# Layer norm's scale, offset and modulation applied where the turned tile is copied; overflow comparison outside its loop; last combine weighed on PE

## The chip, the cores and the metric

The kernel runs on one core of one Trainium2 chip. It is one program of 2,900 lines written engine by engine: TensorE (PE), VectorE (DVE), ScalarE (ACT), GpSimd (POOL) and SyncE (SP) each have their own instruction stream, and they meet at semaphores. The metric is the device time of one execution in microseconds; lower is better. The kernel before takes 4826.23 us, the median of three runs (4824.58 to 4827.52).

## The reference

All data is float32; a sequence of 1024 tokens of width 1024. Two blocks of two layers each follow one another. In the first block a layer is a mixer of delta-rule and gated linear attention heads, a product with `w_out`, and a layer norm. In the second a layer is an attention (a neighbourhood attention, then one with grouped queries), a layer norm, a mixture of 32 experts of which each token uses 2, and a layer norm. What matters here is the norm with the modulation behind it, and how the experts' results are put together:

```python
def layer_norm_2(x, g, b):
    mu = xf.mean(-1, keepdims=True)
    var = jnp.square(xf - mu).mean(-1, keepdims=True)
    return (xf - mu) * lax.rsqrt(var + LN_EPS) * g + b
...
sh1, sc1, g1, sh2, sc2, g2 = jnp.split(mod[:, None, :], 6, axis=-1)
h = x * (1 + sc1) + sh1
y = attention(h)
x = layer_norm_2(ALPHA * x + (1 + g1) * y, ln_g[i, 0], ln_b[i, 0])
h = x * (1 + sc2) + sh2
y = hierarchical_moe(h, ...)        # sum over 2 experts of gate * expert(h)
x = layer_norm_2(ALPHA * x + (1 + g2) * y, ln_g[i, 1], ln_b[i, 1])
```

The reference's experts work on blocks of 128 rows; the kernel gives each expert one block, and the blocks beyond those 32 are overflow.

## The kernel before, in words

`program` calls stage after stage. Each stage is one block in which all engines run their own streams; `end_stage` closes it with a barrier of all engines. The order of the work inside a stage is written out by hand: each engine's loop over the eight token tiles of 128 rows (`order` is 0, 4, 1, 5, 2, 6, 3, 7 in the out stages), and the semaphores between them.

**`out_stage`** runs twice, after each layer of the first block. PE multiplies a tile's mixed heads, already turned (`m.mixT`), with `w_out` in `m.xT` (L1410): 16 products of 128x512, but only 4 for tiles 0 to 3, whose other part was begun in the stage before. The profile shows each such float32 product as two records. DVE adds the tile to `ALPHA * x` (L1466, or L1456 and L1464), takes the moments (L1469, L1472), then computes `(x - mean) * g` (L1476) and `* root + b` (L1479), where the root comes from ACT (L1432, L1434). In the second out stage two more passes give the modulated tile `h = (1 + scale) * x + shift` (L1486, L1488). PE turns the tile of two steps before in eight transposes (L1400, `turn`): `x` in the first out stage, `h` in the second. ACT copies the turned tile from two banks of PSUM to the place of the next stage's operand in two copies of 128x512 (L1425, `copy_out`). There is one pair of banks for turned tiles, so `turn(n)` waits until all of tile n-1's copies are done, and ACT reaches `copy_out(n-2)` only behind the root of tile n:

```python
def turn(n):
    pe.wait_ge(h_done if modulate is not None else x_done, n + 1)
    if n:
        pe.wait_ge(copied, 2 * n)
```

In the first out stage ACT's queue also issues the store of `x` (L1439), behind the wait for DVE's `x_done`.

**`out_route_stage`** runs twice, after the attentions. Its tiles go in order, each with 16 products (L2248); DVE's passes are L2322 to L2345, all four of the norm and the modulation, since the experts gather `h` from DRAM (SP stores it, L2218); in the second layer two more passes scale `x` first (L2317, L2319). PE turns `h` (L2230), ACT copies it (L2274), and PE computes the router's logits from the copy in 8 products of 36 columns (L2239, `route`). PE's order at the end is product 7, turn 6, route 5, route 6, turn 7, route 7; DVE's routing begins at L2359 when all logits are there.

**`experts_stage`** works through 33 fixed blocks. Behind its barrier every engine loads the number of overflow blocks (L2653) and then runs a loop of 15 steps that compares it in each step (L2654). The step's body is one more block of an expert, with a barrier of its own:

```python
with nc.Fori(0, OVERFLOW - 1) as o:
    with nc.If(overflow_blocks > o + 1):
        with nc.Block() as block:
```

**`combine_stage`** follows at once. POOL gathers two rows of results per token from `y_dram` (L2718) into four pairs of buffers, and waits for a pair to come free. ACT weighs the first row with its gate (`weigh`, L2762), DVE adds the second row times its gate (L2812) and `ALPHA * x` (L2815). In the first combine (`columns` is given) the norm's and the modulation's factors are already applied by column: four loads of 128x8 (L2700), a join on DVE (L2847 to L2850), and four activations of 128x256 on ACT (L2769) beside four tensor_scalars on DVE (L2843) out of PSUM. In the last combine PE has nothing to do; ACT sums x (L2774), DVE makes the negative mean (L2828), ACT squares (L2777), takes the root (L2791, L2793), and DVE finishes in two passes (L2834, L2837); SP stores the tile to `out`. `mix(t+1)` stands ahead of tile t's mean, and that ahead of the finish of tile t-1.

## Time and profile before

| what | value |
|---|---|
| median of three runs | 4826.23 us (4824.58 to 4827.52) |
| the profiled execution | 4831.76 us, span of its instructions 4830.0 us |
| PE busy | 4483.6 us, 93% of the span |
| PE loading weights | 2526.0 us, beside it |
| DVE / ACT / POOL busy | 2033.3 (42%) / 1149.8 (24%) / 511.2 us (11%) |
| granted clock of PE, mean | 0.964 |
| DMA | 704 MB, mean 146 GB/s |

The shares are means over more than twenty stages with different limits. In the experts stages (2480 to 3208 us and 4028 to 4757 us) PE is never idle and the weights come at over 330 GB/s; the four norm stages and the combines lie between. A line number leads to a line of the kernel before. Idle time in brackets behind a row is that of the engine just before the instruction, with what ended it.

### The profile page before, as it was taken

The numbers are of one execution on the slowest core, as the hardware profiler recorded it, in microseconds if no ns is written. First come the engines' busy times: TensorE is split into PE (matmuls) and PEld (weight loads), VectorE is DVE, ScalarE is ACT, GpSimd is POOL, SyncE is SP. The second block draws the span as 40 slices with busy tenths as digits, with TensorE's granted clock in tenths as the row PEclk, the third lists the DMA queues.
The fourth block names the chain that finished last, engine by engine and source line by source line (L and its number), as shares of the span: only waits on it lengthen the run. The fifth ranks groups of instructions, "written<-read, shape, count | busy, mean of one in ns | idle before, by whom it ended". The sixth has DMA issues, their size and how long they took to land. (4 is left out here: it accounts for less than half of the span.)

```text
span 4830.0 us, 54241 instructions
## 1 busy us (share of the span) xinstructions
PE 4483.6 (93%) x22194; PEld 2526.0 (52%) x22194; DVE 2033.3 (42%) x2933; ACT 1149.8 (24%) x1919; POOL 511.2 (11%) x348
## 2 busy tenths in 40 slices
PE   7999999899999989998979999968999997999993
PEld 3555664455565456665544444435666654444441
DVE  4555454455555534444431111125666872111113
ACT  2333222234312222222000000013444500000002
POOL 1321110223111000000000000010222000000001
PEclk9999999999999999999979999988999997999997
DMA  3333122233302211111259999950000026999994
GB/s 112 107 104 97 31 79 76 81 105 105 96 27 79 96 42 42 42 39 39 84 208 341 334 336 334 336 181 16 14 14 36 32 85 260 334 336 336 335 333 146
DMA packets 366150, 704.07 MB, mean 146 GB/s; under 512 B 54043, under 2 KB 140195, under 8 KB 365783
## 3 DMA queue, kind: packets, MB, share of 16 engines
q1 hardware_dynamic: 350599, 645.02, 39.0%
q0 software_dynamic: 14112, 51.39, 2.8%
q8 instruction: 179, 2.93, 0.2%
q10 hardware_dynamic: 1200, 4.24, 0.2%
q14 instruction: 60, 0.49, 0.0%
HBM read 630.49 MB, written 70.11 MB: 145 GB/s over the span
## 5 line engine op out<-in xcount | busy, mean ns | idle before, releaser
L2573 DVE TENSOR_TENSOR sb_work<-sb_work,ps 128x512 f32<-128x512 f32 x66 | 45.4, 687 | 863.0 <-PE ps L2492 863.0
L489 PE MATMUL ps<-sb_xT,sb_work 128*128 128x512 f32 x768 | 359.9, 605 | 9.5 <-ACT sb_x_tok L842 5.5
L489 PE MATMUL ps<-sb_mixT,sb_work 128*128 128x512 f32 x768 | 359.6, 605 | 9.5 <-ACT sb_x_tok L842 5.5
L2492 PE MATMUL ps<-sb_work,sb_xT 128*128 128x512 f32 x800 | 354.1, 596 | 0.8 <-DVE sb_xT L2562 0.8
L2492 PE MATMUL ps<-sb_work,sb_mixT 128*128 128x512 f32 x800 | 353.0, 594 | 0.8 <-DVE sb_mixT L2562 0.8
L2568 DVE TENSOR_TENSOR sb_work<-ps,sb_work 128x1024 f32<-128x1024 f32 x66 | 80.8, 1224 | 409.9 <-PE ps L2512 409.9
L1607 PE MATMUL ps<-sb_xT,sb_work 128*128 128x512 f32 x512 | 238.9, 605 | 5.5 <-DMA sb_work<-na_w_qkv 5.5
L2492 PEld LDWEIGHTS ps<-sb_work,sb_xT 128*128 128x128 f32 x800 | 150.4, 191 | 178.4 <-issue 177.2
L2492 PEld LDWEIGHTS ps<-sb_work,sb_mixT 128*128 128x128 f32 x800 | 150.1, 191 | 177.5 <-issue 176.4
L2542 ACT ACTIVATE sb_work<-ps 128x512 f32<-128x512 f32 x66 | 39.4, 597 | 846.1 <-PE ps L2492 846.1
L2512 PE MATMUL ps<-sb_mixT,sb_work 128*128 128x512 f32 x528 | 232.1, 592 | 0.9 <-ACT sb_work L2554 0.9
L2512 PE MATMUL ps<-sb_xT,sb_work 128*128 128x512 f32 x528 | 232.1, 592 | 0.9 <-ACT sb_work L2554 0.9
L489 PEld LDWEIGHTS ps<-sb_xT,sb_work 128*128 128x128 f32 x768 | 137.9, 192 | 148.1 <-issue 130.2
L489 PEld LDWEIGHTS ps<-sb_mixT,sb_work 128*128 128x128 f32 x768 | 138.1, 192 | 147.8 <-issue 129.9
L2095 DVE TENSOR_REDUCE sb_cols<-ps 128x1 f32<-128x1024 f32 x128 | 150.6, 1218 | 85.9 <-PE ps L1938 85.7
L1715 ACT ACTIVATE sb_work<-sb_work,sb_cols 128x512 f32<-128x512 f32 (+1 forms) x128 | 94.8, 741 | 290.4 <-DVE sb_cols L1761 290.4
L1914 PE MATMUL ps<-sb_work,sb_mixT 128*128 128x384 f32 x448 | 154.8, 492 | 3.2 <-PEq L90 3.2
L2512 PEld LDWEIGHTS ps<-sb_xT,sb_work 128*128 128x128 f32 x528 | 97.8, 190 | 112.1 <-issue 111.0
L2512 PEld LDWEIGHTS ps<-sb_mixT,sb_work 128*128 128x128 f32 x528 | 97.8, 190 | 112.1 <-issue 111.0
L1607 PEld LDWEIGHTS ps<-sb_xT,sb_work 128*128 128x128 f32 x512 | 91.8, 191 | 106.1 <-issue 96.9
L2019 ACT ACTIVATE sb_work<-ps,sb_cols 128x1024 f32<-128x1024 f32 x128 | 142.6, 1114 | 17.6 <-DVE sb_cols L2095 12.1
L1948 PE MATMUL ps<-sb_const,sb_work 128*128 128x128 f32 x1024 | 141.8, 281 | 1.9 <-DVE sb_work L2103 0.9
(468 smaller groups left out, 7343.6 us busy)
## 6 DMA issues: line engine op xcount, KB each, us to landing
sb_work<-moe_w_up SPq DMA_DIRECT2D x66, 2048.0 KB, 10.5
sb_work<-moe_w_gate SPq DMA_DIRECT2D x34, 2048.0 KB, 10.6
sb_xT<-moe_w_down SPq DMA_DIRECT2D x33, 2048.0 KB, 10.7
sb_mixT<-moe_w_down SPq DMA_DIRECT2D x33, 2048.0 KB, 10.7
scratch_y<-sb_work SPq DMA_DIRECT2D x82, 512.0 KB, 10.7
sb_xT<-moe_w_gate SPq DMA_DIRECT2D x16, 2048.0 KB, 10.7
sb_mixT<-moe_w_gate SPq DMA_DIRECT2D x16, 2048.0 KB, 10.9
sb_work<-w_in SPq DMA_DIRECT2D x56, 512.0 KB, 3.9
```

The source lines that it names most:

```text
L489: last = pe.matmul(m.ps[:, bank, :], b.w[i][:, k, :], m.xT[:, k, half * HALF:(half + 1) * HALF], start=(k == 0), stop=(k == NK - 1))
L1607: last = pe.matmul(m.ps[:, bank, :], w[j // 2][:, k, :], m.xT[:, k, j % 2 * HALF:(j % 2 + 1) * HALF], start=(k == 0), stop=(k == NK - 1))
L1715: act.activation(p, p, ACT.Exp, bias=top[:, column(i, head)], scale=-1.0, accum_out=total[:, column(i, head)]).then_inc(exponent, 1)
L1914: last = pe.matmul(m.ps[:, bank, 0:WIDE], m.xT[:, k, n * P:(n + 1) * P], w[:, k, :], start=(k == 0), stop=(k == NK - 1))
L1948: last = pe.transpose(m.ps[:, 4 + half, b * P:(b + 1) * P], prob[i % 2][head][:, half * HALF + b * P:half * HALF + (b + 1) * P], ident(m))
L2019: act.activation(prob[i % 2][head], banks(m, 2 * head), ACT.Exp, bias=top[:, column(i, head)], accum_out=total[:, column(i, head)]).then_i ...
L2095: dve.tensor_reduce(top[:, column(i, head)], banks(m, 2 * head), AX.X, ALU.max, negate=True).then_inc(found, 1)
L2492: last = pe.matmul(m.ps[:, 2 + 2 * (n % 2) + part, :], b.x_turned[n % 2][:, k * P:(k + 1) * P], w[:, k, :], start=(k == 0), stop=(k == NK ...
L2512: last = pe.matmul(m.ps[:, 6 + half, :], b.act_turned[n % 2][:, k * P:(k + 1) * P], b.down[n % 2][:, k, half * HALF:(half + 1) * HALF], st ...
L2542: act.activation(b.act[n % 2], m.ps[:, 2 + 2 * (n % 2), :], ACT.Silu).then_inc(silued, 1)
L2568: dve.tensor_tensor(b.y[n % 2], banks(m, 6), b.gate_row, ALU.mult).then_inc(y_copied, 1)
L2573: dve.tensor_tensor(b.act[n % 2], b.act[n % 2], m.ps[:, 3 + 2 * (n % 2), :], ALU.mult).then_inc(multiplied, 1)
```

## The change

Four things are done.

1. In both out stages and both out-and-route stages PE turns the tile that is only normalised, `(x - mean) * root`, one tensor_scalar into a buffer of its own. The norm's gain and offset, and the modulation where there is one, are applied by column while ACT copies the turned tile out of PSUM: eight activations of 128x128 with a scale and a bias column each take the place of two copies of 128x512. The columns are loaded by SP (`load_affine`) and joined on DVE ahead of the first tile's norm (`join_affine`). The untransposed `x`, and `h` where the experts need it, are still computed on DVE, after the normalised tile.
2. In the second out stage `h` is no longer computed apart; the pass count of DVE behind the moments is three there and in the first out stage, five in out-and-route.
3. The number of overflow blocks is compared once, before the loop.
4. In the last combine DVE first writes 16 diagonal matrices with the gates, PE multiplies the gathered rows with them and sums them in PSUM, and DVE adds `ALPHA * x` from there. ACT's weighing and DVE's first pass go; POOL's wait for a free pair is for PE's sum.

```diff
+def join_affine(dve, st, m, modulate, loaded, ready):
+    gain, offset, scale, shift = [m.cols2[:, 8 * n:8 * n + 8] for n in range(4)]
+    dve.wait_ge(loaded, 64 if modulate is not None else 32)
+    if modulate is not None:
+        st.settle(dve.tensor_scalar(scale, scale, 1.0, None, ALU.add))
+        st.settle(dve.tensor_tensor(offset, offset, scale, ALU.mult))
+        dve.tensor_tensor(shift, shift, offset, ALU.add)
+        st.settle(dve.tensor_tensor(scale, scale, gain, ALU.mult))
+    dve.sem_inc(ready, 1)
...
 def out_stage(...)
             load_rows(sp, [(g_row, ln_g), (b_row, ln_b)], rows_loaded)
-            if modulate is not None:
-                load_rows(sp, [(scale_row, modulate[1]), (shift_row, modulate[0])], shift_loaded)
+            load_affine(sp, m, ln_g, ln_b, modulate, columns_loaded)
...
             def turn(n):
-                pe.wait_ge(h_done if modulate is not None else x_done, n + 1)
+                pe.wait_ge(norm_done, n + 1)
                 if n:
                     pe.wait_ge(copied, 2 * n)
-                src = h[n % 3] if modulate is not None else m.x_tok[:, order[n], :]
+                src = normed[n % 3]
...
             def copy_out(n):
                 t = order[n]
+                act.wait_ge(joined, 1)
                 for half in range(2):
                     act.wait_ge(turned, 2 * n + half + 1)
-                    act.copy(m.mixT[:, 4 * half:4 * half + 4, t * P:(t + 1) * P],
-                             chunks(m.ps[:, 6 + half, :])).then_inc(copied, 1)
+                    for k in range(4 * half, 4 * half + 4):
+                        last = act.activation(m.mixT[:, k, t * P:(t + 1) * P], m.ps[:, 6 + half, k % 4 * P:(k % 4 + 1) * P],
+                                              ACT.Identity, bias=shift[:, k:k + 1], scale=scale[:, k:k + 1])
+                    last.then_inc(copied, 1)
...
-                dve.scalar_tensor_tensor(x, x, m.moments[:, t, 0:1], g_row, ALU.subtract, ALU.mult).then_inc(centred, 1)
-                dve.wait_ge(centred, n + 1)
+                if n >= 3:
+                    dve.wait_ge(turned, 2 * (n - 2))
                 dve.wait_ge(root_ready, n + 1)
-                dve.scalar_tensor_tensor(x, x, m.cols[:, t:t + 1], b_row, ALU.mult, ALU.add).then_inc(x_done, 1)
+                dve.tensor_scalar(normed[n % 3], x, m.moments[:, t, 0:1], m.cols[:, t:t + 1], ALU.subtract, ALU.mult).then_inc(
+                    norm_done, 1)
+                dve.wait_ge(norm_done, n + 1)
+                dve.tensor_tensor(x, normed[n % 3], g_row, ALU.mult).then_inc(scaled, 1)
+                dve.wait_ge(scaled, n + 1)
+                dve.tensor_tensor(x, x, b_row, ALU.add).then_inc(x_done, 1)
...
 def experts_stage(...)
-    with nc.Fori(0, OVERFLOW - 1) as o:
-        with nc.If(overflow_blocks > o + 1):
+    with nc.If(overflow_blocks > 1):
+        with nc.Fori(0, OVERFLOW - 1) as o:
...
 def combine_stage(...)
-                    pool.wait_ge(x_mixed, t - 3)
+                    pool.wait_ge(x_mixed if columns is not None else summed, t - 3)
...
             if columns is None:
+                for t in range(NT):
+                    pe.wait_ge(gates_spread, 2 * t + 2)
+                    pe.wait_ge(gathered[t % 4], 32 * (t // 4 + 1))
+                    if t >= 4:
+                        pe.wait_ge(x_mixed, t - 3)
+                    for half in range(2):
+                        for c in range(TOP_K):
+                            last = pe.matmul(m.ps[:, 2 * (t % 4) + half, :], spread_gate[t][c], halves(y[t % 4][c])[half],
+                                             start=(c == 0), stop=(c == TOP_K - 1))
+                    last.then_inc(summed, 1)
                 return
...
+                if columns is None:
+                    dve.wait_ge(summed, t + 1)
+                    dve.scalar_tensor_tensor(x, x, ALPHA, banks(m, 2 * (t % 4)), ALU.mult, ALU.add).then_inc(x_mixed, 1)
+                    return
```

`out_route_stage` is changed as `out_stage` is, with two buffers for the normalised tile; its column loads stand between those of the norm's rows and of the modulation's rows.

On ACT, in the middle of the first out stage, three tiles' roots with the copies between them stand before the change as

```order
L1432 ACTIVATE sb_cols<-sb_moments,sb_eps 128x1
L1434 ACTIVATE sb_cols<-sb_cols 128x1
L1425 COPY sb_mixT<-ps 128x4x128 x2
L1439 DMA scratch_x<-sb_x_tok 128x1024
L1432 ACTIVATE sb_cols<-sb_moments,sb_eps 128x1
```

and now (L1461 and L1463 are the root, L1453 the copies, L1468 the store)

```order
L1461 ACTIVATE sb_cols<-sb_moments,sb_eps 128x1
L1463 ACTIVATE sb_cols<-sb_cols 128x1
L1453 ACTIVATE sb_mixT<-ps,sb_cols 128x128 x8
L1468 DMA scratch_x<-sb_x_tok 128x1024
L1461 ACTIVATE sb_cols<-sb_moments,sb_eps 128x1
```

The place of the copies among roots and stores is the same; two instructions have become eight.

On DVE, at the start of the last combine, the rows are now (L2908 writes the diagonal matrices, L2865 adds PE's sum, L2882 is the mean, L2888 and L2891 finish)

```order
L2908 TENSOR_SCALAR sb_work<-sb_const,sb_gates 128x128 x16
L2865 SCALAR_TENSOR_TENSOR sb_x_tok<-sb_x_tok,ps 128x1024 x2
L2882 TENSOR_SCALAR sb_cols<-sb_cols 128x1
L2865 SCALAR_TENSOR_TENSOR sb_x_tok<-sb_x_tok,ps 128x1024
L2882 TENSOR_SCALAR sb_cols<-sb_cols 128x1
L2888 SCALAR_TENSOR_TENSOR sb_x_tok<-sb_x_tok,sb_cols,sb_work 128x1024
L2891 SCALAR_TENSOR_TENSOR sb_x_tok<-sb_x_tok,sb_cols,sb_work 128x1024
```

The pass that added the second row (L2812 before) is gone, and the 16 small ones stand ahead of everything.

## Rows read from the trace of the kernel before

**Rows 1.** Busy time by stretch: first out stage, first out-and-route, last combine; header names the columns.
```profile
core 0: us, PE busy (x) PEld busy (x) DVE busy (x) ACT busy (x) POOL busy (x), PEclk, DMA share, GB/s
778.90:862.70 83.80, 77.54 (x224) 37.66 (x224) 46.60 (x52) 13.26 (x33) 0.00 (x0) 0.98 0.40 110
2303.00:2444.30 141.30, 137.26 (x448) 74.03 (x446) 72.43 (x74) 12.06 (x33) 0.00 (x0) 0.95 0.27 94
4769.60:4826.10 56.50, 0.00 (x0) 0.00 (x0) 41.80 (x40) 31.17 (x57) 16.11 (x16) 0.50 0.59 214
```

**Rows 2.** Timeline, middle of the first out stage: start us, us, engine, line, operation.
```profile
815.13 3.60 PE L1410 MATMUL ps<-sb_xT,sb_mixT 128*128 128x512 f32 x8
...
817.71 1.05 ACT L1425 COPY sb_mixT<-ps 128x512 f32<-128x512 f32 x2
...
818.91 1.06 PE L1400 MATMUL ps<-sb_const,sb_x_tok 128*128 128x128 f32 x8 [0.18 <-ACT sb_mixT L1425]
```

**Rows 3.** Timeline, tails of the first out stage and of the second.
```profile
856.29 1.05 ACT L1425 COPY sb_mixT<-ps 128x512 f32<-128x512 f32 x2
...
862.06 0.58 ACT L1425 COPY sb_mixT<-ps 128x512 f32<-128x512 f32 x1 [0.27 <-PE ps L1400]
...
1701.02 1.97 PE L1400 MATMUL ps<-sb_const,sb_work 128*128 128x128 f32 x8 [2.56 <-DVE sb_work L1488]
```

**Rows 4.** Timeline, tail of the products of the first out-and-route stage.
```profile
2433.00 1.05 ACT L2274 COPY sb_mixT<-ps 128x512 f32<-128x512 f32 x2
...
2434.11 3.63 PE L2239 MATMUL ps<-sb_work,sb_mixT 128*128 128x36 f32 x16 [3.08 <-ACT sb_mixT L2274]
...
2444.26 0.46 DVE L2359 TENSOR_TENSOR sb_work<-ps,sb_work 128x288 f32<-128x288 f32 x1 [6.47 <-PE ps L2239]
```

**Rows 5.** Groups by form on ACT (count, busy us, mean ns, idle), then a timeline row.
```profile
L991 ACT ACTIVATE sb_work<-sb_work 128x1024 f32<-128x1024 f32 x28 | 29.6, 1057 | 169.4 <-DVE sb_work L1262 169.4
...
L2013 ACT COPY sb_work<-ps 128x512 f32<-128x512 f32 x96 | 56.1, 584 | 153.9 <-PE ps L1948 153.9
...
L1990 ACT COPY sb_work<-ps 128x384 f32<-128x384 f32 x32 | 15.0, 480 | 75.0 <-PE ps L1914 74.9
...
L2798 ACT ACTIVATE sb_x_tok<-sb_x_tok,sb_cols 128x1024 f32<-128x1024 f32 x8 | 9.9, 1241 | 13.6 <-DVE sb_cols L2857 13.6
...
L2769 ACT ACTIVATE sb_mixT<-ps,sb_cols 128x256 f32<-128x256 f32 x16 | 7.7, 560 | 4.3 <-PE ps L2733 4.3
...
3249.35 1.91 ACT L2769 ACTIVATE sb_mixT<-ps,sb_cols 128x256 f32<-128x256 f32 x4
```

**Rows 6.** Groups by form on DVE: a tensor_scalar of 1024 columns.
```profile
L2103 DVE TENSOR_SCALAR sb_work<-sb_work,sb_cols 128x1024 f32<-128x1024 f32 x128 | 107.1, 837 | 4.5
```

**Rows 7.** Chain of waits after the last experts stage; DMA issues, us to landing last.
```profile
4761.23 0.04 POOLq L2654
...
4768.83 0.78 issue
...
sb_cols<-scratch_mods SPq DMA_DIRECT2D x2, 4.0 KB, 4.5
```

**Rows 8.** Timeline of PE in the attention stage before out-and-route.
```profile
2280.32 1.31 PE L1680 MATMUL ps<-sb_work 128*64 128x128 f32 x20 [3.01 <-issue]
...
2286.73 2.40 PE L1680 MATMUL ps<-sb_work 128*64 128x128 f32 x20 [2.80 <-issue]
```

**Rows 9.** Timeline of the last combine: first weighing, one tile's period, last pass.
```profile
4776.05 1.15 ACT L2762 ACTIVATE sb_work<-sb_work,sb_gates 128x1024 f32<-128x1024 f32 x1 [6.02 <-DMA sb_work<-scratch_y,sb_dest]
...
4806.58 1.15 ACT L2777 ACTIVATE sb_work<-sb_x_tok,sb_cols 128x1024 f32<-128x1024 f32 x1 [1.76 <-DVE sb_cols L2828]
...
4812.22 1.15 ACT L2777 ACTIVATE sb_work<-sb_x_tok,sb_cols 128x1024 f32<-128x1024 f32 x1 [1.76 <-DVE sb_cols L2828]
...
4824.76 1.28 DVE L2837 SCALAR_TENSOR_TENSOR sb_x_tok<-sb_x_tok,sb_cols,sb_work 128x1024 f32<-128x1024 f32 x1
```

**Rows 10.** Timeline of PE in the first combine, its first two projections.
```profile
3253.09 6.42 PE L2744 MATMUL ps<-sb_work,sb_mixT 128*128 128x384 f32 x16
...
3260.22 5.33 PE L2744 MATMUL ps<-sb_work,sb_mixT 128*128 128x384 f32 x16
```

More of the change, by code:

```diff
@@ L2271, in copy_out @@
             def copy_out(t):
+                act.wait_ge(joined, 1)
                 for half in range(2):
                     act.wait_ge(turned, 2 * t + half + 1)
[L2274 to L2275 removed]
+                    for k in range(4 * half, 4 * half + 4):
+                        last = act.activation(m.mixT[:, k, t * P:(t + 1) * P], m.ps[:, 6 + half, k % 4 * P:(k % 4 + 1) * P],
+                                              ACT.Identity, bias=shift[:, k:k + 1], scale=scale[:, k:k + 1])
+                    last.then_inc(copied, 1)
             act.preload_act_table_set("natural_log_exp_and_others")
```

73 lines of the change are left out of this document (44 added, 29 removed).

## The prediction

> **What bounds the kernel.** I read the table of stretches first. The program is a string of stages with a barrier after each, so a stage that ends later moves everything behind it by as much. The four stages that end in a layer norm (two out stages, two out-and-route stages) are alike: the first out stage takes 83.8 us, PE busy for 77.5 and DVE for 46.6; the first out-and-route 141.3, PE 137.3 and DVE 72.4, at a granted clock of 0.98 and 0.95 [rows 1]. There PE sets the pace, DVE has room, and what counts is whatever makes PE pause, and the tail behind the last product. Between an experts stage and its combine nothing works for about 8 us, but for an empty loop [rows 7]. In the last combine PE does nothing in 56.5 us, while DVE is busy for 41.8 [rows 1].
>
> Then the timeline. In the middle of an out stage PE's turn of tile 2 in the order (eight 128x128 transposes) starts at 818.91, 0.18 us after ACT's two copies of the turned tile before it, and those start at 817.71, behind the root of the tile just normalised [rows 2]. So the copies are on PE's path wherever a tile of four products stands before the turn. The transposes there read a tile that DVE had long finished. In the tail the chain is root, copy, turn, copy, turn, copy: 856.29 to 862.64 [rows 3]. In out-and-route it is copy, logits, turn, copy, logits [rows 4].
>
> **Part 1: copying with scale and offset.** Two copies of 128x512 become eight activations of 128x128 with a scale and a bias from memory. No such row exists; I build it. A plain copy of 512 columns takes 584 ns, one of 384 takes 480: 0.81 ns a column over a base of 168. An activation of 1024 columns with scale and bias takes 1241 against 1057 without: 184 more. At 256 columns this gives 168 + 208 + 184 = 560, which the row has exactly [rows 5]. So at 128 columns one takes 456 ns. Four of 256 columns, back to back, take 1.91 us: each starts 0.45 after the last, 0.11 less than its duration [rows 5]. Eight of 128 then take 7 x 0.346 + 0.456 = 2.88 us against 1.05, that is 1.83 more. Bounds: 0.35 more if scale and bias cost nothing between neighbours, 2.6 more if none overlap. I take 1.83, by the form nearest to it.
>
> The Trainium skill (ScalarE: Activation LUTs, Rules for kernel authors) budgets 0.3 us for an ACTIVATE with a pointer operand and 0.83 ns an element, an estimate of 0.41 for each, 3.25 for eight: 2.2 more than now. [...] By its rule the sum below would be 4.5 us later.
>
> Where the 1.83 falls:
> - First out stage, middle. The turn at 818.91 and the one at the same place of the next pair start 1.83 later: +3.7.
> - Its tail. Copy at 856.29 ends 859.2; turn to 861.2 (1.97, half clock already, as the second stage's last turn [rows 3], since PE paused longer). DVE writes x later too: after the statistics it waits 0.6 for the root, then one tensor_scalar with columns from memory (0.84, [rows 6], or a little more) and two products or sums of 1.22, so x stands at 859.9 and its DMA issue holds ACT to 860.3. Copy 860.5 to 863.4, turn, its first half at 864.65, copy to 867.5 instead of 862.64: +4.9. Sum of the stage +8.6.
> - Second out stage: the same middle, +3.7; in the tail today's last turn waits for DVE's fourth pass (1701.02 in place of after the copy [rows 3]), which is gone from its path, so three copies and two turns in a row end at 1707.5, not 1703.6: +3.9. Sum +7.6.
> - Out-and-route, each: behind every turn stand sixteen products (four take 3.60, [rows 2]), so only the tail counts. Copy from 2433.00 [rows 4] to 2435.9, logits 3.63, turn 2439.65, first half 1.15 later, copy to 2443.7, logits to 2447.4, DVE at 2447.5 instead of 2444.26: +3.3. In the second such stage likewise: +3.2. That the turn need not wait for the modulated tile gives nothing, for the logits of tile 6 hold PE until then.
>
> Together +22.7, of it about twelve times the 1.83.
>
> DVE itself: one pass fewer in the second out stage, one more in out-and-route (about 10 us a tile, with x scaled first 12.6; PE takes over 17, 141.3 for eight), hidden under PE. The column loads, 128x8 elements each, go ahead of later rows on SP's queue: in the first combine such a load lands in 4.5 us [rows 7]; the first norm of an out stage comes some 6 us after the stage's start and its turn 14 us after that, so they cost nothing. If the cover went, it would be up to 1 us a stage. ACT's and PE's waits for the joined columns are met as early.
>
> **PE's clock.** Each of the four middle pauses grows from 0.18 to 2.0 us. A pause of 0.18 leaves the clock alone. In the attention stage the same line runs 20 matmuls in 1.31 us after a pause of 3.01, but in 2.40 after one of 2.80, 2.4 GHz and 1.2 [rows 8]. So a long pause may or may not bring a stretch at half clock. That row lost 1.1 us to it; for work that goes on behind I take 1.7, an estimate. Bounds 0 and 6.8 for four pauses; I take two of four, +3.4.
>
> **Part 2: the comparison outside the loop.** Nothing overflows (the loop's body has no instruction in the trace): each engine goes 15 times round an empty loop. POOL does so from 4761.23 to 4768.83, 7.6 us, and its gathers, which start the combine, come after it [rows 7]. One comparison remains, 0.3 with its jump: 7.3 saved, twice, -14.6. Bounds 6.0 (a code fetch bared by it) and 7.5. ACT, SP and DVE leave the loop no later than they are needed; PE's own loop, slower, vanishes too, before it has work in the last combine.
>
> **Part 3: last combine on PE.** Today a tile takes 5.64 us (4806.58 to 4812.22): square 1.34, roots 0.5, weighing of tile t+2 by ACT 1.05, two passes of DVE 2.6, mean 0.16, each waiting for the last [rows 9]. Now DVE per tile does: x from PSUM 1.24, mean 0.17, two finishing passes 2.62, with gaps 4.12; ACT sum 1.24, square 1.34, roots 0.5. PE does four 128x512 products, which took 3.60 us at full clock as eight records [rows 2]. DVE bounds, if the clock is granted. PE starts at half clock: in the first combine its first 16 records took 6.42 against 5.33 for the next 16, for full clock came only after some us of steady work [rows 10]. Counted from the landing of the first gather (4776.0 today, [rows 9]): tile 0 is ready at 6.1, tile 1 at 9.6, tile 2 at 13.1; DVE's first mean after that at 14.5, then 4.12 each, last mean (it waits for ACT's sum) at 38.5, two tiles to finish, end at 43.7. Today the end is at 50.04 [rows 9]. So -6.3. Bounds: -8.5 at full clock from the start; the 16 small diagonal matrices (about 0.2 each) hide under the first gather; gathers of tiles 4 to 7 are asked for as PE ends tiles 0 to 3, land about 9 us later, and are due 10 us later: thin, so up to +2.
>
> **Sum**: +22.7 + 3.4 - 14.6 - 6.3 = +5.2 us. The profiled execution took 4831.76; it is 5.5 above the median of the three runs, 4826.23, and I add to the median: 4831.
>
> **Rivals.**
> 1. The copies overlap well, or their operands are free: 0.35 to 1.0 more in place of 1.83, which is 10 to 18 us off: 4813 to 4821. For it: nothing in the rows, no 128-column activation is there. Against: the exact fit at 256. Chance 0.12, somewhat over half of it faster by over 0.2% (9.7 us, about what a measurement of this kernel can tell from no change).
> 2. Slower: eight activations a tile do not overlap, each 0.456, 3.65 for the eight: 2.6 more instead of 1.83. It decides in the turns that wait for them, twelve times: +9.4, so 4841, with all four pauses at half clock 4844. Chance 0.15.
> 3. PE never gets its clock in the last combine: then four products take 6.9 us, over the 5.64 of today, and eight tiles end near 60 instead of 50. +10 instead of -6.3: 4847. Against it: steady work of 6.9 us at a stretch would raise the clock as in the first combine. Chance 0.05. The Trainium skill (TensorE: Matmul & The Clock Gate, A second HAM failure mode) tells of short idle times between groups of matmuls that make the clock swing; at 3.5 us of work in 4.12 the trace has no such case.
> 4. The loop's removal gives nothing, because a jump over the whole body fetches code for as long: +14.6 less, 4846. Against it: each turn of the loop jumps over that body already, in half a microsecond on POOL. Chance 0.03.
>
> The forecast itself has 0.65; its own spread is 4824 to 4838. Range for 8 in 10: 4817 to 4845, which cuts part of rivals 1, 3 and 4. Faster by over 0.2%: 0.10 (0.07 of rival 1, 0.03 of my own). Slower by over 0.2%: 0.24 (rivals 2 to 4 with 0.23, and 0.01 of my own). Within: 0.66.
>
> **What would show it.** Eight activations per tile at 0.45 each, spanning 2.9 us, PE idle about 2.0 us before two turns in each out stage, out stages 7 to 9 us longer, out-and-route 3 longer; gather 1.5 us after the experts' end instead of 8.8; last combine with DVE at 4.1 a tile. If the activations' starts are under 0.25 apart, or the last combine is PE's, I am wrong.

## The result, and the profile after

| | us | runs |
|---|---|---|
| kernel before, beside it | 4825.4 (4822.5 to 4829.0) | 16 |
| changed kernel | 4837.6 (4830.4 to 4841.1) | 16 |
| ratio | 1.0023, 95% interval 1.0016 to 1.0029 | |

The change costs 12.2 us, a quarter of a per cent: slower, by an interval that leaves out 1 and has 0.2% inside it. The forecast was 4831, which is 5.2 over the kernel before, with a range of 4817 to 4845. The time lies in the range. The 7.0 us between 12.2 and 5.2 have a place, and that place was not in the forecast: that the total stayed in the range is in part luck, since the range had been drawn for other things.

The profiled execution of the changed kernel took 4837.7 us, its span is 4835.8. I cut both spans into stages at the first instruction of each (ACT's table load in the norm and combine stages; behind the experts, the load of the number of overflow blocks):

| stages | before | after | difference | forecast |
|---|---|---|---|---|
| out, first and second | 84.9, 89.7 | 95.5, 99.4 | +10.6, +9.7 | +10.3, +9.3 |
| out-and-route, both | 176.9, 174.4 | 179.3, 178.0 | +2.4, +3.6 | +3.3, +3.2 |
| loop behind the experts, both | 8.1, 7.8 | 1.1, 0.5 | -7.0, -7.3 | -7.3, -7.3 |
| first combine | 62.0 | 69.7 | **+7.7** | **0** |
| last combine | 61.3 | 53.2 | -8.1 | -6.3 |
| sum | | | +11.6 | +5.2 |

(In the forecast's column the 3.4 for PE's clock stand with the out stages, 1.7 in each.) The stages in which no code changed differ by -5.8 us in this pair, -4.8 of it in the attention stage ahead of the first out-and-route: 593.4 before, 588.6 after, and 590.8 to 594.3 in the profiles of all kernels below. Without those 5.8 the two spans would lie 11.6 apart, near the 12.2 of the medians. So the 11.6 of the table are taken for what the change does; why one attention stage was short in this one execution is not known, and the same code moves other stages by 1 to 2 us between kernels.

The stretches that answer to [rows 1], same columns:

```profile
778.90:873.30 94.40, 80.12 (x224) 39.11 (x224) 52.16 (x60) 27.85 (x81) 0.00 (x0) 0.92 0.37 98
2318.00:2462.10 144.10, 136.31 (x448) 73.77 (x446) 79.04 (x87) 26.78 (x81) 0.00 (x0) 0.94 0.28 93
4782.60:4835.80 53.20, 29.79 (x64) 12.88 (x64) 33.65 (x48) 23.61 (x49) 15.43 (x16) 0.79 0.66 237
```

In the first out stage ACT is busy for 27.9 us where it was for 13.3: two copies a tile became eight, 48 more instructions. PE does the same 224 matmuls and takes 2.6 us more busy time for them; the other 8 us of the stage it stands still. In the last combine DVE is busy for 33.7 us instead of 41.8, PE for 29.8 instead of nothing.

**The copies.** Group of the activations, then the timeline in the middle of the first out stage, which answers to [rows 2]:

```profile
L1453 ACT ACTIVATE sb_mixT<-ps,sb_cols 128x128 f32<-128x128 f32 x64 | 23.1, 466 | 3.0 <-PE ps L1426 3.0
```
```profile
817.68 2.89 ACT L1453 ACTIVATE sb_mixT<-ps,sb_cols 128x128 f32<-128x128 f32 x8
...
820.72 1.27 PE L1426 MATMUL ps<-sb_const,sb_work 128*128 128x128 f32 x8 [2.02 <-ACT sb_mixT L1453]
...
821.77 15.44 PE L1436 MATMUL ps<-sb_xT,sb_mixT 128*128 128x512 f32 x32
...
843.54 1.07 PE L1426 MATMUL ps<-sb_const,sb_work 128*128 128x128 f32 x8 [2.02 <-ACT sb_mixT L1453]
844.45 13.90 PE L1436 MATMUL ps<-sb_xT,sb_mixT 128*128 128x512 f32 x32
```

Eight copies span 2.89 us (forecast 2.88), and PE's turn waits 2.02 for the last where it waited 0.18. The 32 records of products behind it take 15.44, where the 32 of the next pair (844.45) take 13.90. The stretches around the first say why (columns as above, the clock stands third from the end):

```profile
814.00:820.60 6.60, 4.70 (x17) 2.21 (x15) 5.33 (x7) 3.29 (x10) 0.00 (x0) 1.00 0.33 71
821.70:825.00 3.30, 3.30 (x6) 1.43 (x5) 3.16 (x4) 0.00 (x0) 0.00 (x0) 0.52 0.66 201
825.00:829.00 4.00, 4.00 (x11) 1.82 (x10) 3.20 (x5) 3.30 (x10) 0.00 (x0) 1.00 0.33 69
```

Behind the pause PE runs at half its clock (1.2 GHz) for about 3.3 us. The second such pause of the stage, ahead of 843.54, is as long and leaves the clock at 1.0. In the second out stage it is again one of two (15.25 and 13.90 for the 32 records). Two of four, as the forecast took it; each of the two costs 1.7, with the turn.

The tail, which answers to [rows 3]:

```profile
861.64 2.89 ACT L1453 ACTIVATE sb_mixT<-ps,sb_cols 128x128 f32<-128x128 f32 x8
...
864.67 1.94 PE L1426 MATMUL ps<-sb_const,sb_work 128*128 128x128 f32 x8 [5.45 <-ACT sb_mixT L1453]
...
865.86 2.90 ACT L1453 ACTIVATE sb_mixT<-ps,sb_cols 128x128 f32<-128x128 f32 x8 [1.33 <-PE ps L1426]
...
870.38 2.90 ACT L1453 ACTIVATE sb_mixT<-ps,sb_cols 128x128 f32<-128x128 f32 x8 [1.62 <-PE ps L1426]
```

It begins 5.35 us later than before (two turns at 1.83 and 1.7 for the clock) and is 5.3 us longer from the first copy to the last (11.64 against 6.35).

The tail of the first out-and-route stage, which answers to [rows 4]:

```profile
2447.28 2.89 ACT L2307 ACTIVATE sb_mixT<-ps,sb_cols 128x128 f32<-128x128 f32 x8
...
2461.56 0.46 DVE L2398 TENSOR_TENSOR sb_work<-ps,sb_work 128x288 f32<-128x288 f32 x1 [8.13 <-PE ps L2270]
```

From the copies to the start of DVE's routing it is 14.28 us, before 11.26: 3.0 more (forecast 3.3).

**The loop.** Lines of the chain of waits behind the last experts stage, start, length and what:

```profile
4782.06 0.32 POOLq L2692
...
4782.41 0.06 POOLq L2737
4782.47 0.86 issue
4783.34 0.98 POOL sb_work L2759
```

POOL's load of the number of overflow blocks (L2692) takes 0.32 us, as before the change (L2653 there, 0.31); the 15 turns behind it are gone, and the first gather starts 1.3 us after the load begins.

**The last combine**, answering to [rows 9]:

```profile
4790.39 10.05 PE L2772 MATMUL ps<-sb_work 128*128 128x512 f32 x18 [13.55 <-DMA sb_work<-scratch_y,sb_dest]
...
4796.18 1.22 DVE L2865 SCALAR_TENSOR_TENSOR sb_x_tok<-sb_x_tok,ps 128x1024 f32<-128x1024 f32 x1 [9.93 <-PE ps L2772]
...
4808.33 1.28 DVE L2888 SCALAR_TENSOR_TENSOR sb_x_tok<-sb_x_tok,sb_cols,sb_work 128x1024 f32<-128x1024 f32 x1
...
4812.16 1.28 DVE L2888 SCALAR_TENSOR_TENSOR sb_x_tok<-sb_x_tok,sb_cols,sb_work 128x1024 f32<-128x1024 f32 x1
...
4830.56 1.28 DVE L2891 SCALAR_TENSOR_TENSOR sb_x_tok<-sb_x_tok,sb_cols,sb_work 128x1024 f32<-128x1024 f32 x1
```

A tile takes 3.83 us (4808.33 to 4812.16), all of it DVE; the forecast had 4.12, because it left gaps between DVE's four instructions that are overlaps in truth. From the landing of the first gather (4790.39) to the end of the last pass it is 41.5 us, forecast 43.7, before 50.04.

**The first combine** is where the forecast had nothing. Timeline and DMA issues (the last number is us to landing), to be set beside [rows 7]:

```profile
3232.36 1.28 ACT L2832 ACT_TABLE_LOAD   x1 [13.68 <-PEq L90]
3232.46 0.39 SPq L2741 DMA_DIRECT2D sb_cols<-ln_g  x1
3232.80 0.94 POOL L2759 DMA_INDIRECT sb_work<-scratch_y,sb_dest  x1 [85.71 <-issue]
3232.90 2.02 SPq L2741 DMA_DIRECT2D sb_cols<-ln_b  x1
...
3234.96 3.56 SPq L2741 DMA_DIRECT2D sb_cols<-scratch_mods  x2
...
3240.01 1.15 ACT L2813 ACTIVATE sb_work<-sb_work,sb_gates 128x1024 f32<-128x1024 f32 x1 [6.37 <-DMA sb_work<-scratch_y,sb_dest]
...
3249.49 0.17 DVE L2901 TENSOR_SCALAR sb_cols<-sb_cols 128x8 f32<-128x8 f32 x1 [22.14 <-DMA sb_cols<-scratch_mods]
...
3250.06 1.28 DVE L2868 SCALAR_TENSOR_TENSOR sb_work<-sb_work,sb_gates 128x1024 f32<-128x1024 f32 x1
```
```profile
sb_cols<-scratch_mods SPq DMA_DIRECT2D x2, 4.0 KB, 11.3
sb_cols<-ln_g SPq DMA_DIRECT2D x1, 4.0 KB, 3.3
sb_cols<-ln_b SPq DMA_DIRECT2D x1, 4.0 KB, 6.3
```

ACT has weighed the first gathered row at 3241.2, but DVE's first pass starts at 3250.06: DVE stands in a wait, written ahead of everything else on its queue, for four loads of 4 KB that it needs only for the copies of the turned tiles. The last has landed 17.1 us after the stage's start. In the kernel before the two of `scratch_mods` landed in 4.5 us (now 11.3), the other two in 2.2 and 2.6 (now 3.3 and 6.3), and the wait was over at 6.3 us (DVE's join at 3226.74, stage start 3220.5), ahead of the first gathered row. Before, the first load was issued 0.91 us ahead of the first gather, two of the four stood behind a gather's issue, and all were issued by 3222.8; now the first is 0.34 ahead, three stand behind a gather's, and the last is issued only by 3238.5.

### The profile page after: what moved, and what is told of

The parts are those of the page before. It is cut to its first block and busy times, and to the rows that moved or that the text cites. A ratio compares the mean times of both kernels' runs of the same rounds, so it can differ in the third digit from the quotient of the medians.

```text
span 4835.8 us, 53910 instructions
## 1 busy us (share of the span) xinstructions
PE 4511.2 (93%) x22258; PEld 2537.2 (52%) x22258; DVE 2029.2 (42%) x2969; ACT 1200.5 (25%) x2103; POOL 512.5 (11%) x348
## 5 line engine op out<-in xcount | busy, mean ns | idle before, releaser
L1975 PEld LDWEIGHTS ps<-sb_const,sb_work 128*128 128x128 f32 x1024 | 109.6, 141 | 63.2 <-issue 32.8
## 6 DMA issues: line engine op xcount, KB each, us to landing
sb_work<-moe_w_up SPq DMA_DIRECT2D x66, 2048.0 KB, 10.2
sb_work<-moe_w_gate SPq DMA_DIRECT2D x34, 2048.0 KB, 10.4
sb_xT<-moe_w_down SPq DMA_DIRECT2D x33, 2048.0 KB, 10.6
scratch_y<-sb_work SPq DMA_DIRECT2D x82, 512.0 KB, 10.4
sb_xT<-moe_w_gate SPq DMA_DIRECT2D x16, 2048.0 KB, 10.3
sb_mixT<-moe_w_gate SPq DMA_DIRECT2D x16, 2048.0 KB, 10.6
```

Of the source, the lines that this page charges most:

```text
L1975: last = pe.transpose(m.ps[:, 4 + half, b * P:(b + 1) * P], prob[i % 2][head][:, half * HALF + b * P:half * HALF + (b + 1) * P], ident(m))
```

## The experiments

The theory: (1) the copies cost what the table shows, through ACT's time per tile on PE's path; (2) the loop gives 7.3 at both places, but without it the gathers come earlier beside the column loads of the first combine and slow them, and DVE's early wait for them hands the gain back; (3) the last combine gains 6 to 8. The rivals: that DVE's changed passes cost as much as the copies do; that cutting the copy alone, or its pointer operands alone, costs; that the loads are slow by themselves.

All kernels were timed beside the kernel before, whose median moved between 4825.4 and 4827.8. So a difference between two medians of this table is uncertain by some 2 us unless each is taken against the kernel before that ran beside it; the column "beside" does that. The stages are from one profiled execution each:

| kernel | out | out-and-route | loops | first combine | last combine | total, median | beside | ratio, 95% |
|---|---|---|---|---|---|---|---|---|
| before | 84.9, 89.7 | 176.9, 174.4 | 8.1, 7.8 | 62.0 | 61.3 | 4825.4 | | |
| after | 95.5, 99.4 | 179.3, 178.0 | 1.1, 0.5 | 69.7 | 53.2 | 4837.6 | +12.2 | 1.0016 to 1.0029 |
| 1 copies back | 84.8, 90.0 | 174.8, 174.6 | 0.7, 0.5 | 65.3 | 53.2 | 4805.2 | -22.2 | 0.9941 to 0.9968 |
| 2 loop back | 95.5, 99.1 | 179.9, 178.0 | 10.1, 7.9 | 67.2 | 53.1 | 4853.7 | +26.3 | 1.0043 to 1.0070 |
| 3 last combine back | 95.5, 99.3 | 180.0, 178.0 | 1.0, 0.6 | 65.4 | 60.7 | 4843.1 | +15.7 | 1.0021 to 1.0048 |
| 4 late join | 95.5, 99.2 | 177.7, 177.5 | 1.0, 0.5 | 59.8 | 53.7 | 4830.8 | +3.4 | 0.9999 to 1.0017 |
| 5 gathers wait | 95.5, 99.1 | 179.9, 177.9 | 1.0, 0.5 | 66.3 | 53.4 | 4835.9 | +8.2 | 1.0009 to 1.0027 |
| 6 plain copies | 87.8, 90.1 | 175.0, 175.3 | 1.0, 0.5 | 65.9 | 53.6 | one run | | |
| 7 wide copies | 87.6, 90.0 | 175.1, 175.1 | 0.7, 0.6 | 69.1 | 52.9 | one run | | |
| 8 copies shared | 91.2, 95.2 | 178.0, 177.5 | 0.7, 0.5 | 66.2 | 53.2 | 4827.4 | +2.1 | 0.9997 to 1.0015 |
| 9 copies back, late join | 84.9, 89.8 | 176.2, 174.5 | 0.7, 0.6 | 60.5 | 53.4 | 4806.3 | -21.4 | 0.9940 to 0.9967 |
| 10 as 9, PE warmed | 84.9, 89.8 | 176.3, 174.7 | 0.7, 0.5 | 60.2 | 51.1 | **4801.9** | -23.4 | 0.9936 to 0.9963 |
| 11 as 10, early join | 84.9, 89.8 | 176.3, 174.5 | 0.7, 0.5 | 69.9 | 51.2 | 4804.9 | -20.5 | 0.9940 to 0.9967 |

### 1. The norm stages as before

`out_stage` and `out_route_stage` are the old functions; the core of it:

```diff
-                    for k in range(4 * half, 4 * half + 4):
-                        last = act.activation(m.mixT[:, k, t * P:(t + 1) * P], m.ps[:, 6 + half, k % 4 * P:(k % 4 + 1) * P],
-                                              ACT.Identity, bias=shift[:, k:k + 1], scale=scale[:, k:k + 1])
-                    last.then_inc(copied, 1)
+                    act.copy(m.mixT[:, 4 * half:4 * half + 4, t * P:(t + 1) * P],
+                             chunks(m.ps[:, 6 + half, :])).then_inc(copied, 1)
```

> The out stages and the out-and-route stages are those of before; the loop's comparison and the last combine stay changed. Theory A: the profiles lay 10.6 and 9.7 us on the two out stages and 2 to 3.5 on each out-and-route stage, all through the eight activations (12 times 1.83 us) and pauses of PE that cost its clock. Undone, 22 to 26 us come back: 4812 to 4816 us, 9 to 14 under before. Rival B: part of that is the column loads and DVE's reordered passes, or the difference lies in other stages; then less than 18 us come back, 4820 or more.

Measured 4805.2 (4802.7 to 4805.8, 5 runs): 32.4 below the changed kernel (34.4 beside), more than either expectation had. The four stages give 28.0 of it; 4.4 more come from the first combine, whose column loads landed earlier in this kernel. The part of the change that rewrote the norm stages is a plain loss of 26 to 28 us by the stages, and the rest of the change by itself is a gain of half a per cent.

### 2. The loop back

```diff
-    with nc.If(overflow_blocks > 1):
-        with nc.Fori(0, OVERFLOW - 1) as o:
+    with nc.Fori(0, OVERFLOW - 1) as o:
+        with nc.If(overflow_blocks > o + 1):
```

> The comparison stands inside the loop again; the copies and the last combine stay changed. Theory A: in the last combine the 7.3 us of the loop come back in full (to 7.8 less what the gathers hid), but in the first combine its removal gained next to nothing, because the column loads of that stage had an issue 0.9 us ahead of POOL's first gather behind the loop and only 0.3 now, and land in 11.3 us in place of 4.5; so the total rises by 6 to 9 us only: 4844 to 4847 us. The landing of the column loads is back at 4 to 5 us. Rival B: the late landing comes from something else (what the DMA queues hold from the stage ahead), the loop's removal gains 7.3 twice, and its return costs 14 to 15: 4852 us, with the column loads still landing after 10 us or more.

Measured 4853.7 (4851.5 to 4858.1, 5 runs), 16.1 above the changed kernel (14.1 beside). The loops come back with +9.0 and +7.4. The first combine falls by 2.5 only and not to 62, for the loads are as slow as in the changed kernel; the join is done 15.6 us into the stage:

```profile
sb_cols<-scratch_mods SPq DMA_DIRECT2D x2, 4.0 KB, 12.4
```

So theory A of this experiment missed, and what rival B had forecast came: a total near 4852 with loads that land after 10 us or more (B's reason, what the DMA queues hold from the stage ahead, no run tests). In this build POOL issues its first gather 1.55 us ahead of SP's first load, where in the kernel before it came 0.91 behind, with the same loop. The loop's presence does not bring the quick landing back, and part (2) of the theory is not shown as it stands: the late landing cannot be laid on the missing loop alone.

### 3. The last combine back

The old `combine_stage`: in the last combine ACT and DVE weigh the two rows, and PE does nothing.

> Both combines are those of before; the copies and the loop's comparison stay changed. Theory A: the last combine is 8 us longer without PE (41.5 us from the first gather's landing to DVE's end become 50): 4845 to 4847 us. Rival B: the gathers of tiles 4 to 7, asked for earlier with PE, or the final stores take part of it back, and the difference is under 5: 4842 or less.

Measured 4843.1 (4839.6 to 4844.5, 5 runs), +5.5 (+3.5 beside), between the two expectations. The stage itself goes from 53.2 to 60.7, +7.5; the first combine fell by 4.3 in the same kernel (join at 13.3 us into the stage, not 17.1), which is the same code in both. Sum +3.2 by these two rows. The stage's gain of 7.5 to 8.1 is confirmed; the total mixes it with the landing of the loads.

### 4. The join late

The four small DVE instructions and their wait go from the head of DVE's queue in the first combine to behind the third tile's offset, ahead of the first copy that needs them:

```diff
-            if columns is not None:
-                dve.wait_ge(columns_loaded, 64)
...
-                dve.tensor_tensor(shift, shift, ln_b, ALU.add).then_inc(columns_ready, 1)
+                    if t == 2:
+                        dve.wait_ge(columns_loaded, 64)
...
+                        dve.tensor_tensor(shift, shift, ln_b, ALU.add).then_inc(columns_ready, 1)
+                        dve.wait_ge(columns_ready, 1)
```

> As the change, but in the first combine DVE joins the columns only ahead of its first copy out (tile 2 of the loop), not ahead of its first pass. Theory A: DVE stood 9 us at the column loads with the first tile's rows there since 3241.2; now it starts at ACT's weighing, and the first combine is 6 to 8 us shorter: 4830 to 4832 us. Rival B: the column loads are late because all transfers are; the gathers bound the stage, and the time stays within 2 us of 4837.6.

Measured 4830.8 (4825.4 to 4833.5, 11 runs), 6.8 below the changed kernel (8.8 beside), as theory A had it. DVE's first pass starts right behind ACT's weighing, and the stage takes 59.8 us in place of 69.7:

```profile
3241.70 1.28 DVE L2868 SCALAR_TENSOR_TENSOR sb_work<-sb_work,sb_gates 128x1024 f32<-128x1024 f32 x1 [13.90 <-ACT sb_work L2813]
```

This is the place of the forecast's miss: with the wait out of the way the kernel is 3.4 us over the kernel before, where the forecast had 5.2. (Its last combine is 1.3 us better than forecast, which is part of the rest.)

### 5. The gathers wait for the loads

```diff
+            if columns is not None:
+                pool.wait_ge(columns_loaded, 64)
             for t in range(NT):
```

> The changed kernel, but in the first combine GpSimd waits until the four column loads have landed before it issues its first gather. Theory A, the loads are slow there because the gathers' packets run beside them: alone they land some 5 to 6 us after the stage's first instruction (4.5 us from issue to landing in the kernel before), the first gather starts then and needs the 7.2 us up to ACT's weighing that it needs now, so the first pass on DVE starts about 14 us into the stage in place of 17.6, and the stage takes 66 us in place of 69.7: total 4833 to 4836. Theory B, the loads are slow by themselves or by the weight loads that SP issues behind them: they land at about 17 us as now, the gathers start only there, and the stage takes 76 us or more: total 4842 or more.

Measured 4835.9 (4832.2 to 4840.9, 11 runs), 1.7 below the changed kernel (4.0 beside); the stage takes 66.3 us, as theory A had it (DVE's first pass starts 15.5 us into it; 14 was expected). Timeline and DMA issues:

```profile
3237.39 1.28 ACT L2834 ACT_TABLE_LOAD   x1 [13.68 <-PEq L90]
...
3240.03 1.32 SPq L2741 DMA_DIRECT2D sb_cols<-scratch_mods  x2
3241.39 2.58 SPq L176 DMA_DIRECT2D sb_work<-gqa_w_qkv  x3
3243.37 0.17 DVE L2903 TENSOR_SCALAR sb_cols<-sb_cols 128x8 f32<-128x8 f32 x1 [10.98 <-DMA sb_cols<-scratch_mods]
...
3251.73 1.15 ACT L2815 ACTIVATE sb_work<-sb_work,sb_gates 128x1024 f32<-128x1024 f32 x1 [13.06 <-DMA sb_work<-scratch_y,sb_dest]
...
3252.91 1.28 DVE L2870 SCALAR_TENSOR_TENSOR sb_work<-sb_work,sb_gates 128x1024 f32<-128x1024 f32 x1 [8.83 <-ACT sb_work L2815]
```
```profile
sb_cols<-scratch_mods SPq DMA_DIRECT2D x2, 4.0 KB, 2.6
```

Without gathers beside them the two loads that took 11.3 us land in 2.6, though SP's weight loads follow them as before. So the gathers slow them. How much they do so is set beside the head start of the loads here:

| kernel | first load ahead of first gather by | scratch_mods loads land in | join, us into the stage |
|---|---|---|---|
| 5 gathers wait | no gather till landed | 2.6 | 6.0 |
| before | 0.91 | 4.5 | 6.3 |
| 11 early join | 0.67 | 10.1 | 17.2 |
| 1 copies back | 0.66 | 7.6 | 12.5 |
| 9 late join | 0.66 | 5.8 | later by design |
| after | 0.34 | 11.3 | 17.1 |
| 6 plain copies | 0.34 | 8.7 | 14.1 |
| 3 last combine back | 0.34 | 7.9 | 13.3 |
| 4 late join | 0.34 | 7.5 | later by design |
| 7 wide copies | 0.33 | 10.4 | 16.7 |
| 2 loop back | -1.55 | 12.4 | 15.6 |

The largest head start goes with the quickest landing beside gathers and the smallest with the slowest, but in between it decides nothing: at 0.66 to 0.67 us the loads land in 5.8, 7.6 and 10.1, at 0.34 in 7.5 to 11.3. Why the kernel before has 4.5 and none of the others does beside gathers stays open. The Trainium skill (DMA: Bandwidth & Descriptors, Queues, rings and completion order) says that each DMA engine takes turns between its queues packet by packet. From that rule one would infer that a load of 1024 single elements, which is many small pieces, waits for its turns beside a gather's rows of 4 KB. The rows here agree in direction (2.6 us alone, 4.5 to 12.4 beside gathers); the turns themselves no run here shows.

### 6. Eight plain copies

```diff
-                        last = act.activation(m.mixT[:, k, t * P:(t + 1) * P], m.ps[:, 6 + half, k % 4 * P:(k % 4 + 1) * P],
-                                              ACT.Identity, bias=shift[:, k:k + 1], scale=scale[:, k:k + 1])
+                        last = act.copy(m.mixT[:, k, t * P:(t + 1) * P], m.ps[:, 6 + half, k % 4 * P:(k % 4 + 1) * P])
```

> The changed kernel with its eight copies of 128x128 a tile in the four norm stages as plain copies: scale, offset and modulation are left out of the turned tile, so what is computed behind them is another thing, and only the out stages' lengths are read. Theory A, the price of a copy is the instruction's fixed part plus the two pointer operands: a plain 128x128 copy takes 0.25 to 0.30 us in place of 0.466, eight of them 1.5 to 2.2 us in place of 2.90, and each out stage is 3 to 6 us shorter than the 95.5 and 99.4 us of the changed kernel. Theory B, it is the cutting into eight alone: a plain copy of 128x128 takes 0.40 us or more, and the out stages stay within 1.5 us of the changed kernel's.

```profile
815.03 1.43 ACT L1453 COPY sb_mixT<-ps 128x128 f32<-128x128 f32 x8
...
816.60 1.06 PE L1426 MATMUL ps<-sb_const,sb_work 128*128 128x128 f32 x8 [0.55 <-ACT sb_mixT L1453]
```

This kernel leaves the scale and the offset out, so its values are others, and only its stages are read. A plain copy takes 0.25 to 0.35 us, eight span 1.43 in place of 2.89. PE's pause is 0.55 and the turn behind it takes 1.06, as at full clock. The out stages take 87.8 and 90.1 us, 7.7 and 9.3 less than the changed kernel's: theory A's direction, and more than the 3 to 6 it expected.

### 7. Two wide copies with pointers

```diff
-                    for k in range(4 * half, 4 * half + 4):
-                        last = act.activation(m.mixT[:, k, t * P:(t + 1) * P], m.ps[:, 6 + half, k % 4 * P:(k % 4 + 1) * P],
-                                              ACT.Identity, bias=shift[:, k:k + 1], scale=scale[:, k:k + 1])
+                    last = act.activation(m.mixT[:, 4 * half:4 * half + 4, t * P:(t + 1) * P], chunks(m.ps[:, 6 + half, :]),
+                                          ACT.Identity, bias=shift[:, 0:1], scale=scale[:, 0:1])
```

> The changed kernel with two copies of 128x512 a tile in the four norm stages, each with scale and bias from one column of four (scale and offset of the other three columns are left out, so only the stages' lengths are read). If cutting the copy into four is what costs, and not its operands (A), a copy takes about the 0.58 us of the plain one before plus 0.1 to 0.2 us, two of them 1.2 to 1.5 us in place of 2.90, and each out stage takes within 2 us of the 84.9 and 89.7 us of the kernel before. If the pointer operands or DVE's changed passes cost (B), the out stages stay over 88 and 93 us.

```profile
817.28 1.43 ACT L1452 ACTIVATE sb_mixT<-ps,sb_cols 128x512 f32<-128x512 f32 x2
...
818.86 1.06 PE L1426 MATMUL ps<-sb_const,sb_work 128*128 128x128 f32 x8 [0.56 <-ACT sb_mixT L1452]
```

This kernel takes one column's scale and offset for four, so its values are others too. A copy takes 0.767 us against 0.585 for the plain one before, and the two span 1.43 us, by chance the span of the eight plain ones; the out stages are alike to 0.2 us as well. The first out stage, 87.6, lies between the two expectations (under 86.9 for A, over 88 for B), the second, 90.0, is A's. So neither half alone is the cost. Cutting in eight costs 0.38 a tile (1.43 against 1.05), the pointers on two copies cost 0.38, and together they cost 1.84, because the pointers' 0.18 us is paid per instruction: eight times. DVE's three passes are in all of kernels 6 and 7. With them and copies of 1.43 the out stages are 2.7 to 2.9 and 0.3 to 0.4 us over the kernel before, so DVE's passes explain at most that, of the 10.6 and 9.7.

### 8. The copies shared by ACT and DVE

```diff
+                for k in range(4, 8):
+                    last = dve.tensor_scalar(m.mixT[:, k, t * P:(t + 1) * P], m.ps[:, 7, (k - 4) * P:(k - 3) * P],
+                                             scale[:, k:k + 1], shift[:, k:k + 1], ALU.mult, ALU.add)
+                last.then_inc(copied, 1)
```

ACT keeps k = 0 to 3; DVE does this right behind the pass that writes the normed tile, in the two out stages.

> The changed kernel with the eight affine copies of a turned tile in the two out stages shared: four on ACT, four on DVE right behind its pass that writes the normed tile. Theory A, the path through the tile's copies sets these stages: ACT's half takes 1.45 us in place of 2.90, DVE's half starts 0.8 us later and is done about 2.2 us after ACT's begin (and in the tail, where DVE is free, after 1.5 us), so each out stage takes 91 us (now 95.5) and 94 us (now 99.4) and the total falls by 8 to 12 us to 4825 to 4830. Theory B, DVE's passes are what the stages wait for as much: four more instructions of about 0.27 us a tile on DVE cost what ACT gives back, and the stages stay within 2 us.

```profile
814.96 1.49 ACT L1452 ACTIVATE sb_mixT<-ps,sb_cols 128x128 f32<-128x128 f32 x4
...
815.91 1.36 DVE L1487 TENSOR_SCALAR sb_mixT<-ps,sb_cols 128x128 f32<-128x128 f32 x4
817.43 1.06 PE L1426 MATMUL ps<-sb_const,sb_work 128*128 128x128 f32 x8 [1.45 <-DVE sb_mixT L1487]
```

Measured 4827.4 (4820.9 to 4833.9, 11 runs), 10.2 below the changed kernel (10.1 beside); stages 91.2 and 95.2, expected 91 and 94. The pause is 1.45 in place of 2.02, now with DVE as the last. Theory A holds: DVE had the room, and the path through the copies sets the stage. The interval of the ratio, 0.9997 to 1.0015, holds 1, so the 12 us are mostly made up for (3.5 of it stand in the first combine, 66.2, and not in the copies); but the two wide plain copies of kernel 1 are still better by 11.6 us in these two stages.

### 9 to 11. The parts that gain, together

Kernel 9 is kernel 1 with the late join.

> The parts that gained together: copies of the norm stages as before, comparison outside its loop, last combine weighed on PE, and in the first combine DVE's join of the columns moved behind the third tile. From the run with the copies back (4805.2 us, first combine 65.3 us) the first combine goes to the 59.8 us that the late join gave: 4799 to 4801. Rival: the attention behind it or its loads take the gain up, 4803 or more.

Measured 4806.3 (4803.7 to 4806.8, 5 runs), where kernel 1 had 4805.2. The stage did fall, from 65.3 to 60.5, but the total did not follow: a miss, and the number that the rival had. In the two profiles the other stages differ by up to 2.4 us each with the same code (start of the program +2.4, first out-and-route +1.4, first experts +1.0, the attention behind the first combine +1.1), so 4.8 us in a stage lie close to what one pair of builds can show.

Kernel 10 adds work for PE while it waits for the first gather of the last combine:

```diff
             if columns is None:
+                for _ in range(6):
+                    pe.matmul(m.ps[:, 7, :], ident(m), m.x_tok[:, 0, 0:HALF], start=True, stop=True)
                 for t in range(NT):
```

> The best kernel so far with the late join (4806.3 us), and six matmuls of 128x512 that PE does in the last combine before the first gather has landed; their result is written over. PE's granted clock was at half until 4.3 us behind the landing, where the products of the first tiles take 1.22 us in place of 0.59. Theory A, the work before them gives the clock, the first tile reaches DVE 1.3 to 2.5 us sooner, and the stage takes 51 to 52 us in place of 53.4. Theory B, DVE starts as late, because the clock comes no sooner or the warm-up itself runs past the landing: 53.0 us or more.

```profile
4746.59 7.55 PE L2753 MATMUL ps<-sb_x_tok,sb_const 128*128 128x512 f32 x12 [6.24 <-PEq L90]
...
4753.98 11.32 PE L2761 MATMUL ps<-sb_work 128*128 128x512 f32 x26
...
4757.61 1.22 DVE L2854 SCALAR_TENSOR_TENSOR sb_x_tok<-sb_x_tok,ps 128x1024 f32<-128x1024 f32 x1 [8.15 <-issue]
```
```profile
4753.90:4765.30 11.40, 11.40 (x28) 5.11 (x27) 3.26 (x4) 3.92 (x8) 6.37 (x8) 1.00 0.98 367
```

The six matmuls, twelve records, end as the gather lands. Measured 4801.9 (4799.1 to 4802.7, 5 runs), the fastest: 23.4 us or half a per cent under the kernel before. The first products run at full clock, at once: in the 11.4 us behind the landing PE's granted clock is 1.00, where in the changed kernel the first 4.3 us ran at half. DVE starts 3.6 us after the products' start instead of 5.8, and the stage takes 51.1 us instead of 53.4. Beside the kernel before, kernel 10 is 2.0 us better than kernel 9, which is what the stage gives.

Kernel 11 is kernel 10 with the join at the head again.

> The same six matmuls, with the join of the columns at the start of the first combine as in the changed kernel. If the 4.8 us that the late join took off the first combine's stage reach the end of the kernel, this is 4 to 5 us above the run beside it with the late join; if the attention behind the stage takes them up again, the two are within 1 us of one another.

Measured 4804.9, but over 4798.9 to 4811.6 in 5 runs. The profiled execution, span 4809.1, has the first combine at 69.9 us against 60.2. The median lies 3.0 above kernel 10's, which is between the two expectations; what is plain is the spread, 12.7 us against 3.6. Only a long landing (10.1 us) was profiled, so that the spread is the landing's doing is a guess: kernel 4, with the late join, spreads over 8.1 us in 11 runs.

## Why the prediction came out as it did

By its own steps:

- **Copies, +22.7.** Right: an activation 0.466 us (forecast 0.456), eight in 2.89 (2.88), two middle turns and two tails per out stage as worked out. With the clock's 3.4 the forecast was 26.1, the table has 26.3. Kernels 6 and 7 show that the sum was made of the right pieces: 0.18 for the two pointers, per instruction. The Trainium skill (ScalarE: Activation LUTs, What ACT_TABLE_LOAD costs) gives 186 ns and 0.833 ns an element with immediates, 93 ns for each pointer operand and 93 of overlap between neighbours. An estimate from that page for this form is 479 ns and a start every 386. The trace has 466 and a start every 346 ((2.89 - 0.466) / 7), so the overlap here is 120 ns and the trace decides.
- **PE's clock, +3.4.** Right in size, two pauses of four, by a choice in the middle of bounds and not by a rule: pauses of one length did and did not lose it. The 1.7 for one loss had no row behind it either, only the 1.1 of [rows 8]; the traces have 1.7 for each. Both halves of this term were guessed well, which is luck.
- **Loop, -14.6, and the first combine at nothing.** The loops are gone as forecast (-14.3). The step that failed is the sentence behind it, "ACT, SP and DVE leave the loop no later than they are needed", together with the one on the column loads, which let the landing of 4.5 us [rows 7] stand as a property of the load. In the changed kernel the loads landed in 11.3 us, and DVE's wait for them, which had been free, became the last to end. That is +7.7: 6.9 until DVE's first pass (17.7 us into the stage against 10.8), the rest in the stage behind it, where the first products at the start of the projections took 7.20 us instead of the 6.42 of [rows 10]. That the wait is the place is shown by kernel 4, that gathers beside the loads slow them by kernel 5. That the loop's removal is what made them slow is not shown: with the loop back they landed in 12.4 (kernel 2), and with the norm stages or the last combine back in 7.6 and 7.9 (kernels 1 and 3). No single part of the change, undone, brings the 4.5 back. The forecast took a landing seen once, beside gathers, for a fixed price.
- **Last combine, -6.3.** Right mechanism, size -8.1. The period is 3.83 and not 4.12, since DVE's instructions overlap a little where gaps had been put; PE's late clock came as forecast and cost 2.1 to 2.3 us, by kernel 10.
- **Rivals.** 1 and 2 fell with the span of 2.89 us. 3 did not come, PE's clock rose 4.3 us after its first product. 4 did not come. A fifth case, the one that moved the result, was not among them: the forecast had named it as a cover ("if the cover went, it would be up to 1 us a stage") in the out stages, priced too low, and not asked it of the combine, where the wait stands at the head of DVE's queue.

## To carry to other kernels

An activation of ACT with per-partition operands pays for them once per instruction: before a copy is split so that each piece has its own column, multiply the operands' price (0.18 us here) by the pieces, and look whose turn waits for the last piece. When dead time ahead of a stage is removed, go through every engine's first wait in that stage and ask whether its cover was that dead time; put waits for small loads where their data are used, not at the head of a queue, and keep loads of single elements away from gathers. Where PE has to start with its clock down and waits anyway, try filler matmuls in the wait. And take each median against the kernel before that ran beside it: 2 us of drift between two sets of runs are as large as some of the parts here.

## What the runs showed that I had not expected

- A 4 KB load of single elements landed in 2.6 us with no gather beside it and in 4.5 to 12.4 with gathers, and nearly the same order of issue gave 5.8, 7.6 and 10.1.
- The moment at which SP and POOL enter a stage moves against one another between builds (from 0.91 us apart to 1.55 the other way with the same loop), and a wait that was covered in one build stood bare by 9 us in another.
- Six filler matmuls of 128x512 (7.55 us) bought 2.3 us in a stage that is bound by DVE, because DVE waits there for the first tile only.
- Two kernels whose copies differ in kind (eight plain, two wide with pointers) but span the same 1.43 us had the same out stages to within 0.2 us: by these two it is the span of a tile's copies that the stages feel, and not their kind or number.
